# Two places in a TensorE instruction stream: where two value products stand among the attention scores, and where the last transposes stand among dense products

## The reference, cut to what matters

```python
q = q.reshape(B, nb, BLOCK, N_KV_HEADS, GROUP, HEAD_DIM)
...
s = jnp.einsum('bnqkgd,bnskd->bnkgqs', q, kb).astype(jnp.float32) * (HEAD_DIM ** -0.5)
...
probs = jax.nn.softmax(jnp.concatenate([s, sink], axis=-1), axis=-1)[..., :-1]
o = jnp.einsum('bnkgqs,bnskd->bnqkgd', probs.astype(vb.dtype), vb)
```

## Time and profile before

| | |
|---|---|
| time, median of 3 | 1082.36 us (1082.12 to 1082.36) |
| time of the profiled execution | 1082.2 us |
| its span | 1080.4 us |
| granted TensorE clock | 0.999 |
| TensorE matmuls busy | 1073.4 us, 99% of the span |
| TensorE weight loads busy | 878.9 us, 81% |
| VectorE, ScalarE, GpSimd busy | 79%, 46%, 35% |
| share of TensorE in the chain that ended last | 97% |

### The profile page before, as it was taken

How to read it: one execution, slowest core, us unless ns; L and a number is a source line. 1 busy time by engine, 2 the same in 40 slices (tenths; PEclk the granted TensorE clock), 3 DMA queues, 4 the chain that set the end, 5 groups by cost and what they waited for, 6 DMA issues and landing times.

```text
span 1080.4 us, 17124 instructions
## 1 busy us (share of the span) xinstructions
PE 1073.4 (99%) x6368; PEld 878.9 (81%) x6368; DVE 857.9 (79%) x1219; ACT 494.2 (46%) x961; POOL 377.6 (35%) x303
## 2 busy tenths in 40 slices
PE   8999999999999999999999999999999999999998
PEld 7888888888888888888777777888888888888887
DVE  5988998989999895776799987567669777376775
ACT  6543353443334444632666665434437335344332
POOL 1058888887778879753100001000000000000000
PEclk9999999999999999999999999999999999999999
DMA  9802231421334243649788786555545743334655
GB/s 358 353 1 79 74 122 43 145 88 40 127 108 146 78 124 111 245 154 251 204 229 207 210 210 218 190 173 177 176 134 196 255 156 117 98 118 140 205 179 195
DMA packets 65598, 173.88 MB, mean 161 GB/s; under 512 B 6777, under 2 KB 15737, under 8 KB 63193
## 3 DMA queue, kind: packets, MB, share of 16 engines
q1 hardware_dynamic: 39088, 100.11, 27.7%
q10 hardware_dynamic: 22976, 51.78, 14.5%
q0 software_dynamic: 3456, 20.97, 7.6%
HBM read 133.29 MB, written 55.41 MB: 175 GB/s over the span
## 4 chain that ended last, share of the span: by engine, by line
PE 97%; DVE 1%; ACT 1%; DMA 0%; issue 0%; ACTq 0%; DVEq 0%
PE psg L1002 37%; PE psg L786 24%; PE psb L1289 13%; PE psg L1200 7%; PE psg L817 2%; PE psb L1069 1%; PE psg L905 1%; PE psg L1289 1%; PE psg L994 1%; PE psg L1144 1%; PE psb L1230 1%; PE psg L1230 1%; PE psg L851 1%; PE psg L1242 1%; PE psg L1087 1%; PE psb L905 1%
## 5 line engine op out<-in xcount | busy, mean ns | idle before, releaser
L1347 POOL TENSOR_TENSOR pair_w<-early_raw,pair_w 128x512 fp32r<-128x512 f32 x143 | 192.8, 1357 | 90.5 <-ACT pair_w L1557 90.5
L1002 PE MATMUL psg<-early_hi,pair_w 128*128 128x512 f32 x672 | 207.0, 389 | 0.0
L1002 PE MATMUL psg<-h_hi,pair_w 128*128 128x512 f32 x504 | 155.2, 389 | 0.0
L1557 ACT ACTIVATE pair_w<-early_raw 128x512 fp32r<-128x512 f32 x143 | 87.1, 627 | 134.1 <-POOL early_raw L1363 90.7
L1002 PEld LDWEIGHTS psg<-early_hi,pair_w 128*128 128x128 f32 x672 | 126.1, 188 | 26.2
L2237 DVE SCALAR_TENSOR_TENSOR psb<-conv,cols,psb 128x510 f32<-128x510 f32 (+6 forms) x196 | 137.6, 744 | 0.0
L1002 PE MATMUL psg<-early_lo,pair_w 128*128 128x512 f32 x336 | 130.7, 389 | 0.0
L1002 PEld LDWEIGHTS psg<-h_hi,pair_w 128*128 128x128 f32 x504 | 94.6, 188 | 19.7
L1330 POOL TENSOR_TENSOR rstd<-mean_sq,expo 128x4 f32<-128x4 f32 x3 | 3.1, 1021 | 297.8 <-DVE mean_sq L2040 278.8
L1002 PE MATMUL psg<-h_lo,pair_w 128*128 128x512 f32 x252 | 98.0, 389 | 0.0
L2026 DVE TENSOR_TENSOR w_lo<-w_raw,w_hi 128x1024 fp32r<-128x1024 f32 x49 | 60.0, 1225 | 40.2 <-ACT w_hi L1468 36.9
(11 more groups left out here) (370 smaller groups left out, 2422.0 us busy)
## 6 DMA issues: line engine op xcount, KB each, us to landing
w_raw<-weights SPq DMA_DIRECT2D x52, 512.0 KB, 3.6
gates<-ring ACTq DMA_DIRECT2D x30, 512.0 KB, 3.6
w_sums<-w_pairs POOLq DMA_DIRECT2D x12, 1024.0 KB, 8.7
ring<-gates ACTq DMA_DIRECT2D x24, 512.0 KB, 4.2
early_raw<-w_pairs SPq DMA_DIRECT2D x11, 1024.0 KB, 5.5
early_raw<-w_pairs SPq DMA_DIRECT2D x11, 768.0 KB, 4.4
block_raw<-w_sums SPq DMA_DIRECT2D x32, 256.0 KB, 3.1
block_raw<-w_pairs SPq DMA_DIRECT2D x24, 256.0 KB, 3.6
```

The costliest lines, as they stand in the source:

```text
L1002: mm = nc.tensor.matmul(bank, pair_w[:, at_w, w, k * P:(k + 1) * P], r[:, k, :], start=(not onto and k == 0 and m == 0), stop=(k == KP - 1 ...
L1347: nc.gpsimd.tensor_tensor(pair_w[:, at_w, 1, :], early_source(s, n), pair_w[:, at_w, 0, :].bitcast(F32), ALU.subtract).then_inc(early_spli ...
L1557: nc.scalar.activation(pair_w[:, early_slot(b), 0, :], early_source(s, n), ACT.Copy).then_inc(early_split_hi, 1)
```

## The change

Two edits in TensorE's list. No instruction is added or taken away.

The crossed outputs stood between the first eight scores (`j2` = 0) and the last eight (`j2` = 1) of `scores(p, 1)`. Now they stand ahead of the last two of the first eight: those of `sub` = 3.

The transposes `turn(LAST_P)` stood directly behind `outputs(LAST_P - 1)`, ahead of step 2 of the first dense tile. Now they stand ahead of step 4: six dense matmuls lie between.

```diff
                 for j2 in range(2):
-                    if (jp, j2) == (1, 1) and p > 2:
-                        crossed_outputs(p - 2)
                     for sub in range(1 if n == 0 else P // SUB):
+                        if (jp, j2, sub) == (1, 0, P // SUB - 1) and p > 2:
+                            crossed_outputs(p - 2)
                         for par in range(2):
...
             def attention_end(h, j, k):
                 if (h, j, k) == (0, 0, 2):
                     outputs(LAST_P - 1)
+                elif (h, j, k) == (0, 0, 4):
                     turn(LAST_P)
                 elif (h, j, k) == (0, 1, 2):
                     outputs(LAST_P)
```

## The result

The changed kernel takes 1083.70 us (median of 22), the kernel before 1082.24 us (22 runs beside them): a ratio of 1.0012, 95% interval 1.0007 to 1.0018. It is about 1.5 us slower (1083.70 - 1082.24). The profiled execution's span went from 1080.4 to 1082.0 us. Of the executions behind this document one was left out of its ratio: one of the eleven of the first experiment took 3594 us, which moves that median by 0.04 us.

What follows compares the result with a forecast made beforehand. The prediction took TensorE, busy for 99% of the span, to bound the kernel. The first edit's +1.6 us and the second's -0.6 gave +1.0 on a profiled 1082.2: forecast 1083.4 us, range 1080.8 to 1084.6.

Steps and rivals of the forecast that it cites:

- the strict order: Rival: attention matmuls start strictly in list order, last straight pass 0.20 us late a phase, +2.0 in all, 1084.4 us; chance 0.15.
- the listed wait: Straight outputs (L1144) waiting for the end of the crossed outputs (L1123): 0.18 us in each of 13 phases, 2.4 us.
- The eighths work through lists of their own: In attention, each eighth of TensorE's array starts its next small matmul when free; the two left idle finish late.
- ScalarE's bound: Crossed outputs can't start before ScalarE empties the gate half, which ends 0.05 us ahead of their first weight load.
- The step: First edit: in an ordinary phase the two idle eighths make the transposes 0.09 to 0.15 us later, taken as 0.12.
- The sum of +1.6: First edit's total loss over the attention: 12 x 0.12 + 0.18 = 1.6 us, bounds 1.3 and 2.0.
- 12 x 0.12: The part of the first edit's loss from 12 ordinary phases, transposes 0.12 us later in each.
- the price of two interruptions from three rows: End of attention: one interruption costs 3.32 us now; split, outputs alone 1.81 and transposes alone 0.85; 0.6 us won.
- The 0.04 us for a second restart: Second edit: after each restart some ten dense matmuls run at 0.23 us instead of 0.2265, 0.04 us more.
- The idle time at L1743: Sign: in each phase crossed loads start 0.05 us after ScalarE's end, with an idle time listed (L1742 in the prediction).
- The other signs: Eighth crossed start at 0.35 to 0.41, uneven straight rounds near 577.1, transposes at 2.76 us, no L1717 wait, another dense gap.

Runs made afterwards that it cites:

- the first experiment: The first edit alone against the kernel before, crossed outputs ahead of the round's last two scores, last transposes where they were: 1084.22 us, ratio 1.0019.
- the late quarter first: Against the changed kernel, crossed outputs of the quarter whose scores are postponed issued first of the eight instead of fourth and eighth: 1082.74 us.
- four scores ahead: Against the changed kernel, the crossed outputs stand ahead of the last four scores of the round instead of the last two: 1083.45 us.
- a whole round ahead: Against the kernel before, the second edit plus crossed outputs moved a whole round of eight scores ahead: 1084.83 us, ratio 1.0026.
- the semaphore in two parts: Against the second edit alone, `crossed` sent once behind each side's four crossed matmuls, each side's straight outputs waiting for their own: 1082.02 us.

## Why the prediction was right, point by point

**The direction and the place.** The forecast was 1083.4 us, 1.0 over the median before; measured is 1083.70, 1.46 over the runs beside it. The total alone decides little: it lies halfway between the forecast's +1.0 and the +2.0 of the strict order, and the traces have to tell the two apart. "No change that one would call measurable" was put too low: with 22 runs on each side the interval of 1.0007 to 1.0018 tells 0.12% from none. The first edit costs and the second wins, as worked out, and the listed wait vanished while the phases grew.

**The eighths work through lists of their own.** This carried the forecast. The changed kernel shows scores that start behind straight outputs, and crossed outputs that start at 0.78 and 0.83 while six others start from 0.84 on. The run with the late quarter first and the one with four scores ahead settle it. In all three the transposes follow the crossed output of the last idle eighth at the same distance: 0.763 and 2.717, 0.809 and 2.761, 0.829 and 2.780 us, that is 1.95 us each time.

**Strict order, the rival with 0.15.** It had the crossed outputs all at 0.84 or later and 0.20 us a phase. The trace shows two that start ahead of that. Each starts 0.002 to 0.004 us behind its own weight load, the fourth and the eighth of the list, and the record that sends `crossed`, the second pass of the eighth, is the twelfth of sixteen to start. So the strict order is refuted for matmuls that go to different eighths. The rule of the Trainium skill that the forecast weighed ("TensorE: Matmul & The Clock Gate", Part 3, strict FIFO in start and end) does not hold in this form here: in the changed kernel the crossed outputs that are fourth and eighth in the list start first, at 0.78 and 0.83 us on the phase's clock, and the six others from 0.84 on.

The prediction was wrong to say that the trace before can't tell. Its rounds don't go through the eighths in one order: scores go quarter by quarter with both halves of the rows, crossed outputs half by half with all four quarters. In each of the 12 ordinary phases there, the eight starts of the crossed outputs, sorted by time, lie 0.135 or 0.136 us behind the eight starts of the round of scores ahead, sorted by time, and that is what a pass of a score holds its eighth. So each starts when its own eighth comes free. Kept to the order of the list, the fifth could not start ahead of the fourth, which has to wait for the last quarter. The record that sends `crossed`, last in the list, starts 1 ns ahead of another or together with it. In phase 3, where all eighths are idle, it is the last. The nanoseconds could have ruled the strict order out before the forecast.

**ScalarE's bound.** It was read from a distance of 0.05 us between two rows with no wait listed. The run a whole round ahead shows it as a wait of 0.33 us. The traces show it without that run as well: in all 13 phases the first crossed load starts 0.051 or 0.052 us behind ScalarE's end in the kernel before, and 0.050 to 0.053 in the changed kernel, with the late quarter first and four scores ahead, however early the load is issued.

**The size of the first edit.** The step put 0.12 us (0.09 to 0.15) on each ordinary phase. To the transposes it is 0.14. Another 0.02 us of the phase's 0.16 (9.107 against 8.947) lies behind them, in the dense matmuls. The forecast had nothing for that. It isn't the edit's: with the first edit alone the dense stretch of a phase is as long as before (5.66 us), in the changed kernel's trace it is 5.68. What makes these restarts slower stays open. Phase 3 was put at 0.18; from its first crossed output to the transposes it became 542.706 - 541.134 = 1.57 us, against 542.396 - 541.008 = 1.39 before, so 0.18 as foreseen. The sum of +1.6 measured +2.1 in the trace, of which the term "12 x 0.12" is 12 x 0.14 and the unforeseen part some 0.25.

**The size of the second edit.** Forecast 0.6, measured 0.65 (92.47 to 91.82): the price of two interruptions from three rows was right. In the changed kernel the outputs alone take 2.26 us and the transposes alone 1.30 us from the dense start ahead to the second one behind, 1.81 and 0.85 without two pitches each, as in the forecast. The 0.04 us for a second restart was hardly there. What lies behind it moved as foreseen: masks at 664.22, 2 us ahead of need, and the last low part through at 672.21, over 1 us ahead of the dense half that wants it.

**What I had said one would see.** The idle time at L1743 in every phase is not there: the loads stand behind a semaphore instruction (L1117), and their gap of 0.05 us is too short to be listed. The other signs are.

**What the forecast left on the table.** The second edit alone is the better kernel, 1081.6 us with either three or six dense matmuls.

## What to carry to other kernels

What follows is shown for this kernel alone. Small matmuls that share the array should go round its parts evenly between two waits. One that is held back ahead of a wait leaves its part idle and makes the whole array late at the next change of shape, even where the list of waits then looks cleaner. Before work is moved ahead of a wait, look whether the thing waited for is ready at the new place; a release 0.05 us ahead of the load it frees shows in no list and is the bound all the same. And when a short group waits for a copy of what was just computed, put a few dense matmuls between, as many as the copy takes; here six did no better than three.

## What the runs showed that I had not expected

A semaphore on the last matmul of the list isn't sent by the last one to start. In the changed kernel `crossed` is sent by a record with four others behind it, up to 0.02 us later, and the semaphore for the second half of the scores by a record that starts 0.05 us ahead of the last score's second pass. Nothing comes of it here: a straight output starts only when its own eighth is free, and VectorE takes the second half at 578.81, 0.8 us behind the start of that last pass (578.01). Where a reader follows at once, an order that leaves parts of the array out of step would have to be looked at for this.

Which instruction carries a wait seems to count: with the wait that ends last in an instruction of its own ahead of the load, the first matmul came 0.03 us (the semaphore in two parts) and 0.05 us (a whole round ahead) later than with the wait on the load itself. No run moved the wait and nothing else.

And the dense matmuls behind the transposes restart at slightly different speeds from kernel to kernel (5.66 or 5.68 us for the same 24 in a phase), in lists that are the same there; with the late quarter first and a whole round ahead they differ from phase to phase as well (5.65 to 5.69). Why stays open.
